# The delta-rule inverse and chunk loop of a two-block decoder, with TensorE's products, one low part and the gate products in another order

## The reference

```python
def step(state, inp):
    r_t, k_t, v_t, w_t, a_t, b_t = inp
    sa = jnp.einsum('bhvk,bhk->bhv', state, a_t)
    state = state * w_t[:, :, None, :] + sa[..., None] * b_t[:, :, None, :] + v_t[..., None] * k_t[:, :, None, :]
    return state, jnp.einsum('bhvk,bhk->bhv', state, r_t)
...
y = head_norm(y, gn_gain.reshape(H, N), RWKV_GN_EPS)
bonus = jnp.sum(rh * kh * r_k[None, None].astype(jnp.float32), axis=-1, keepdims=True) * vh
return (y + bonus).reshape(B, S, W) * g          # g = sigmoid(g_lo) @ g_up
```

## Time and profile before

| | us |
|---|---|
| median of three runs | 1006.78 |
| lowest, highest | 1005.49, 1008.01 |
| the profiled execution | 1008.22 |
| its span, first to last instruction | 1006.4 |
| TensorE busy in the span | 874.4 |
| VectorE busy | 451.5 |
| ScalarE busy | 331.8 |
| GpSimd busy | 17.4 |
| mean DMA rate over the span | 292 GB/s |

### The profile page before, as it was taken

The page is one execution under the profiler, slowest core; times in us unless marked ns, Lnnn a source line. Parts: engine busy times, 40 slices in busy tenths (PEclk is TensorE's granted clock), DMA queues, the critical chain, the costliest instruction groups (busy, mean ns, idle before and its releaser), DMA issues.

```text
span 1006.4 us, 16152 instructions
## 1 busy us (share of the span) xinstructions
PE 874.4 (87%) x6998; PEld 603.9 (60%) x6998; DVE 451.5 (45%) x579; ACT 331.8 (33%) x433; POOL 17.4 (2%) x34
## 2 busy tenths in 40 slices
PE   9999999999999999999899988666866776686785
PEld 7889988888888889989888633121312212131232
DVE  6776778678776448897766311000100000010002
ACT  6476664665555328645433300000000000000002
POOL 0420000000000000000000000000000000000000
PEclk9999999999999999999999999787979879789798
DMA  9894324576645455452369999999999999999995
GB/s 324 247 360 136 141 87 167 167 254 211 200 168 190 186 168 209 146 189 85 109 195 344 391 411 398 428 428 428 428 429 427 428 428 429 427 430 429 423 425 226
DMA packets 75968, 294.34 MB, mean 292 GB/s; under 512 B 5247, under 2 KB 32655, under 8 KB 62592
## 3 DMA queue, kind: packets, MB, share of 16 engines
q1 hardware_dynamic: 70352, 283.91, 72.5%
q10 hardware_dynamic: 4128, 6.34, 1.8%
q0 software_dynamic: 1424, 3.16, 1.1%
HBM read 290.25 MB, written 4.10 MB: 292 GB/s over the span
## 4 chain that ended last, share of the span: by engine, by line
PE 63%; DMA 28%; DVE 5%; issue 2%; SPq 1%; ACT 1%; DVEq 0%; ACTq 0%
DMA arena<-in_w_down 10%; DMA arena<-in_w_gate 9%; DMA arena<-in_w_up 8%; PE psum L1262 8%; PE psum L1950 8%; PE psum L1125 6%; PE psum L1126 6%; PE psum L1127 6%; PE psum L1289 4%; PE psum L1264 4%; PE psum L1978 3%; PE psum L1628 2%; PE psum L1162 1%; PE psum L1161 1%; PE psum L1159 1%
## 5 line engine op out<-in xcount | busy, mean ns | idle before, releaser
L1950 PE MATMUL psum<-arena,featL 128*32 128x512 f32 x1008 | 158.7, 697 | 58.4 <-DMA arena<-in_w_up 33.3
L2525 DVE TENSOR_TENSOR ring_rounded<-arena,hi_rounded 128x2048 fp32r<-128x2048 f32 x76 | 173.6, 2289 | 59.8 <-ACT hi_rounded L2077 58.6
L2077 ACT ACTIVATE hi_rounded<-arena 128x2048 fp32r<-128x2048 f32 x76 | 144.8, 1912 | 85.2 <-PE psum L1127 22.3
L1950 PEld LDWEIGHTS psum<-arena,featL 128*32 128x32 f32 x1008 | 37.7, 124 | 167.2 <-issue 86.6
L1262 PE MATMUL psum<-ffn_in_rounded,hi_rounded 128*128 128x512 f32 x352 | 122.4, 394 | 0.7 <-DVE ffn_in_rounded L2517 0.7
L1978 PE MATMUL psum<-arena,featT 128*32 128x512 f32 x424 | 79.1, 729 | 37.6 <-DMA arena<-in_w_down 33.2
L1125 PE MATMUL psum<-hi_rounded,featT_rounded 128*128 128x256 f32 (+1 forms) x336 | 104.1, 310 | 3.1 <-DVE featL_rounded L2567 2.2
L1127 PE MATMUL psum<-hi_rounded,featL_rounded 128*128 128x256 f32 (+1 forms) x336 | 101.8, 303 | 0.0
L1126 PE MATMUL psum<-ring_rounded,featT_rounded 128*128 128x256 f32 (+1 forms) x336 | 101.8, 303 | 0.0
L1264 PE MATMUL psum<-ffn_in_rounded,ring_rounded 128*128 128x256 f32 x352 | 97.5, 277 | 0.0
L1262 PEld LDWEIGHTS psum<-ffn_in_rounded,hi_rounded 128*128 128x128 f32 x352 | 66.0, 187 | 16.2 <-DVE ffn_in_rounded L2517 1.0
(11 more groups left out here) (367 smaller groups left out, 1278.7 us busy)
## 6 DMA issues: line engine op xcount, KB each, us to landing
arena<-in_w_down SPq DMA_DIRECT2D x32, 2048.0 KB, 17.1
arena<-in_w_gate SPq DMA_DIRECT2D x28, 2048.0 KB, 21.0
arena<-in_w_up SPq DMA_DIRECT2D x24, 2048.0 KB, 23.3
arena<-in_w_in SPq DMA_DIRECT2D x14, 2048.0 KB, 8.6
arena<-in_w_up SPq DMA_DIRECT2D x25, 1024.0 KB, 8.4
arena<-in_w_gate SPq DMA_DIRECT2D x14, 1024.0 KB, 5.5
arena<-in_w_down SPq DMA_DIRECT2D x7, 1024.0 KB, 10.8
arena<-in_w_out SPq DMA_DIRECT2D x3, 2048.0 KB, 8.2
```

Of the source, the lines that this page charges most:

```text
L1950: ins = mm(psum[32 * j:32 * j + 32, MB[4 + m], :], xg[:, 4 * half + k, 32 * j:32 * j + 32], weights(m, half, j, 512 * k), start=half == 0 ...
L2077: fn(high, view, ACT.Copy).then_inc(hi_ready, 1)
L2525: tt(low, view, high.bitcast(F32), ALU.subtract).then_inc(lo_ready, 1)
```

## The change

It computes the same values. TensorE's order and the fill list are written anew between 467 and 530 us, and what ACT, DVE and SP do about those fills follows.

- `natl A` (eight transposes) moves from the start of mixing to between Re and Ro; `gn` moves from behind Q to behind Aak; Q moves from before TT to behind it. AakT gets another place in SBUF (`AakT = P2`, in featT).
- `u_inner(1)` and `u_inner(2)`, and `y_rows(0)` and `y_rows(1)`, are merged so that products of the two chunks alternate. `mT 0 0` moves from before `u_inner(0)` to behind `u_state(1)`, `mT 1 0` from before `u_state(3)` to behind the last `y_rows`.
- The low part of the second `wo2` chunk is made by GpSimd.
- `gated_bonus` for both t and `gated_gain(0)` stand before the loop, `gated_gain(1)` in its first turn. `low_moved` of `mT 0 0` stands in turn 1, that of `mT 1 0` behind `rw_square(1)`, and ACT's `y_moved(1)` and `high_moved` of `mT 1 0` stand before its first `root`.
- The pieces that SP loads wait for other fills.

```diff
 (fill list)
+BETWEEN = {"H3": (("mat", "Aak"), ("gn",)), "N": (("mat", "Re"), ("natl", "A"), ("mat", "Ro")), "TT": (("Q",),)}
 (SP)
-                    first_load(NQ, 0, ("inv", "N", 1), ("mat", "Ro", 1), *inv(("HT", 0), ("HT", 1)))
+                    first_load(NQ, 0, ("gn", 1), ("inv", "N", 1), ("mat", "Ro", 1), ("inv", "HT", 1))
...
-                    first_load(3, 2, ("St", 0), ("U", 1, 1), ("St", 1), ("U", 2, 1))
+                    first_load(3, 2, ("U", 1, 1), ("St", 1), ("U", 2, 1), ("St", 2))
 (GpSimd)
+            g = chunk_of[("wo2", 0), 1]
+            pool.wait_ge(hi_ready, g + 1)
+            pool.wait_ge(lo_ready, g)
+            high, view, low = hi_view(g)
+            ptt(low, view, high.bitcast(F32), ALU.subtract).then_inc(lo_ready, 1)
 (TensorE)
+                if name == "H3":
+                    mat("Aak")
+                    for t in range(NT):
+                        b = begin("gn", t)
+                        pe.wait_ge(lora_act, 2)
+                        end(mm(b, sig_g[:, t * P:(t + 1) * P], gup[:], start=True, stop=True))
+                if name == "N":
+                    mat_both("Re", 0)
+                    for t in range(NT):
+                        transposes(("natl", "A", t), [At[:, k, t * P:(t + 1) * P] for k in range(4)],
+                                   lambda: pe.wait_ge(rw_ready, 1))
+                    mat_both("Ro", 1)
...
+                for i in range(4):
+                    for par in range(2):
+                        for c in chunks:
+                            t, r, to, h = c // 2, head_rows(c % 2), head_rows(1 - c % 2), 2 * i + par
+                            ins = mm(banks[c][par][to, 64 * i:64 * i + 64], TT[r, t, 4 * par + i, :], Qn[r, t, 64 * h:64 * h + 64],
...
             state(0)
-            u1 = u_inner(1)
-            u2 = u_inner(2)
+            u1, u2 = u_inner(1, 2)
             u_state(u1, 1)
+            transposes(("mT", 0, 0), mixed_rows(0, 0), lambda: pe.wait_ge(mixed_ready, 1))
+            state(1)
             y0 = [begin("Y", 0, par) for par in range(2)]
-            y_rows(y0, 0)
-            state(1)
             y_state(y0, 1, True)
             u_state(u2, 2)
-            y_rows(y0, 1)
+            u3, = u_inner(3)
             state(2)
-            u3 = u_inner(3)
-            transposes(("mT", 1, 0), mixed_rows(1, 0), lambda: pe.wait_ge(mixed_ready, NT))
+            y_rows(y0, 0, 1)
             u_state(u3, 3)
...
             y_rows(y1, 3)
+            transposes(("mT", 1, 0), mixed_rows(1, 0), lambda: pe.wait_ge(mixed_ready, NT))
 (ScalarE)
                 if c == 2:
                     y_moved(0)
-                    high_moved("mT", 1, 0)
+            y_moved(1)
+            high_moved("mT", 1, 0)
             root(48, RW_H, 64, 2)
-            y_moved(1)
             high_part(first["wo2", 0] + 2, ("Y", 1, 1))
 (VectorE)
-                    low_part(chunk_of[("wo2", 0), 1])
...
+            gated_bonus(0)
+            gated_bonus(1)
+            gated_gain(0)
             for c in range(NCH):
...
                 if c < NCH - 1:
+                    if c == 1:
+                        low_moved("mT", 0, 0)
                     if c:
                         link(tt(S[c + 1], S[c], bc(PC[:, :, c], 64), ALU.mult))
                     wait_filled(dve, "St", c)
...
                     if c == 0:
                         empty(nc.vector.tensor_copy(S[1], b), "St", 0)
-                        gated_bonus(0)
+                        gated_gain(1)
...
-            gated_bonus(1)
             rw_square(0)
-            gated_gain(1)
             rw_scale(0)
             rw_square(1)
+            low_moved("mT", 1, 0)
             rw_scale(1)
```

More of the change, by code:

```diff
@@ L266, in plan_fills @@
     add("act", "p2", 3, 1)
-    for t in range(NT):
-        add("act", "natl", "A", t)
     for j in range(3):
@@ L1521, in _ @@
             tokens_late(("p2", 3, 1), ("p2", 3), 1)
-            for t in range(NT):
-                transposes(("natl", "A", t), [At[:, k, t * P:(t + 1) * P] for k in range(4)], lambda: pe.wait_ge(rw_ready, 1))
             for j in range(3):
@@ L1708, in y_state, with y_rows @@
                             ins.then_inc(y_first, 1)
[L1710 to L1712 removed]
+            def y_rows(banks, *chunks):
                 for name in ("Re", "Ro"):
                     wait_emptied(pe, "mat", name, 1)
[L1715 to L1717 removed]
+                for c in chunks:
+                    u_known(c)
+                    if c:
+                        pe.wait_ge(y_first, 2 * c)
                 for i in range(4):
                     for par in range(2):
[L1720 to L1724 removed]
+                        for c in chunks:
+                            t, both, h = c // 2, (Re, Ro)[c % 2], 2 * i + par
+                            ins = mm(banks[par][head_rows(c % 2), 64 * i:64 * i + 64], both[:, t, 4 * par + i, :],
+                                     VU[c][:, 64 * h:64 * h + 64], start=c == 0 and i == 0, stop=True, skip_group_check=True)
+                            if c % 2 and i == 3:
+                                end(ins)
             u_inner(0)
@@ L2327, in _ @@
             ret_move(3, 1)
-            for t in range(NT):
-                wait_filled(act, "natl", "A", t)
-                empty(fn(natl["A"][:, t, :], bank("natl", "A", t), ACT.Copy), "natl", "A", t)
             high_part(first["wo2", 0], ("p2", 3, 1))
@@ L2363, in _ @@
                     high_part(first["wo2", 0] + 1, ("p2", 3, 1))
+                if name == "H3":
+                    for t in range(NT):
+                        wait_filled(act, "gn", t)
+                        empty(fn(gnat[:, t, :], bank("gn", t), ACT.Copy), "gn", t)
                 if name == "N":
                     root(48 + RET_H, RET_H, RET_D, 1)
+                    for t in range(NT):
+                        wait_filled(act, "natl", "A", t)
+                        empty(fn(natl["A"][:, t, :], bank("natl", "A", t), ACT.Copy), "natl", "A", t)
                 if name == "TT":
-                    high_moved("mT", 0, 0)
-                if name == "G2":
                     for t in range(NT):
@@ L2371, in _ @@
                         empty(fn(Qn[:, t, :], bank("Q", t), ACT.Copy), "Q", t)
-                    for t in range(NT):
-                        wait_filled(act, "gn", t)
-                        empty(fn(gnat[:, t, :], bank("gn", t), ACT.Copy), "gn", t)
             def y_moved(t):
@@ L2927, in _ @@
                     merge()
-                for e in INV_EXTRA.get(name, ()):
-                    for par in range(2):
-                        masked(extra[e][0], e, extra[e][1], par)
+                for key in BETWEEN.get(name, ()):
+                    if key[0] == "mat":
+                        dst, m = extra[key[1]]
+                        for par in range(2):
+                            masked(dst, key[1], m, par)
+                        if key[1] == "Re":
+                            ret_scale(0)
                 if name == "H3":
```

89 lines of the change are left out of this document (29 added, 60 removed).

## The result

The changed kernel takes **1009.24 us** (median of 14 runs, 1007.75 to 1011.27), the kernel before 1007.12 (14 runs beside them, 1005.49 to 1008.84). The ratio is 1.002, with a 95% interval of 1.0011 to 1.0028: some 2 us slower. The forecast was 1006.0 with a range up to 1008.6. So the two traces end at the same time, and the difference has to be read from where each stage starts.

The account below looks back on a forecast made before the run. The prediction took the experts' weight transfers as the bound, released by mixed_ready = 4 and the wo2 fills. Terms -1.1 (issue), -0.6 (mT 0 0), +0.25 (loop), +0.7 (end of mixing) gave -0.75, or -0.8 us: 1006.0, range 1003.4 to 1008.6.

Parts of the forecast that it names:

- What bounds the kernel: Experts' weight transfers bound the end; it moves only with mixed_ready = 4 and the end of the wo2 fills.
- The issue waits: -1.1: In the inverse: light work moved among the products saves 1.1 us of TensorE's 3.52 us of instruction waits; bounds 0 and 3.5.
- The count by blocks of 4.15 us: In the inverse: instructions arrive in blocks of some 127 products with weight loads, one per 4.15 us at best.
- rival 2: In the inverse: the issue waits only move, saving 0, sum +0.3, 1007.1 us; chance 0.10.
- the 0.55 near Re: In the inverse: third of five issue waits, to vanish since gn, N and Re take 5.0 us, above 4.15.
- the 0.32 and the 0.46: In the inverse: first and last of five issue waits; 0.32 was to stay, 0.46 to stay as 0.3 to 0.5.
- mT 0 0 leaves: -0.6: Before the loop: removing mT 0 0's transposes saves 0.6 us; with the issue waits the loop starts at 513.35 us.
- The loop: +0.25: Chunk loop: alternating saves 0.6 and 0.6, a new 1.2 us wait before u_state(2) takes it; 0.25 us longer.
- The end of mixing: +0.7: From u_state(3): VectorE waits 2.4 us for ACT's root; 0.7 given back, mixed_ready = 4 comes 0.75 earlier.
- The wo2 products see the same: In the wo2 stage: despite waiting for mT 1 0's low part, the first fill ends 0.7 to 0.8 us earlier.
- rival 3: In the wo2 stage: TensorE's clock falls to half behind a 2.6 us wait, 3.0 us lost, 1009.0; chance 0.05.
- Rival 4: Beside H2 and H3: GpSimd's low part holds VectorE up, at most 3.5 us lost, 1009.5; chance 0.05.

Follow-up runs that it names:

- before_mt: Kernel before with only mT 1 0's transposes, high part and low part moved to the end of mixing as in the change; ratio 1.0007.
- tail_loop: Changed kernel with t = 0's root first, mT 1 0's low part right behind t = 0's scaling, mT 0 0 behind state(1), its low part behind the state sum; ratio 1.0001.
- late_pieces: Changed kernel with SP's 1-MB pieces of experts' weights held back until U of the last chunk is full; 1017.12 us.
- gate_alt: Kernel before with the gate products moved from behind U3, and u_inner(1, 2) and y_rows(0, 1) alternating, u_inner(3) ahead of state(2); ratio 0.9991.
- changed_again: The changed kernel itself run once more, unaltered, against the kernel before; ratio 1.0019.
- filler9: Changed kernel with 9 products of no use put into TensorE's stop of 2.53 us in the wo2 stage; ratio 1.0004.
- low_first: Changed kernel with VectorE's low part of mT 1 0 moved ahead of the scaling of t = 0; ratio 1.0010.
- gate_tail: gate_alt with mT 1 0's transposes behind the last y_rows, t = 0's root first on ACT, mT 1 0's low part right behind t = 0's scaling; ratio 0.9970.
- gate_tail_shift: gate_tail with one of SP's 1-MB loads, (2, 2), moved from beside TT and Q to behind load (3, 1); ratio 0.9964, 1004.05 us.

## Why the prediction was wrong, step by step

**What bounds the kernel: right, and not followed to its end.** I named two events, mixed_ready = 4 and the end of the fills. The runs speak for the second as the mark: the change and before_mt are early at the first (0.23, 1.16 us) and late at the second (1.58, 0.66), and neither is faster. It is no perfect mark: tail_loop is early at both and its median is not, and from the second issue to the end of the span the 17 traces of the table take 458.8 to 462.5 us.

**"The issue waits: -1.1": wrong.** The count by blocks of 4.15 us gave each stretch the same supply. It forecast 0.1 each for TT and Q; Q had 1.48 and state(0) 0.79 and 0.23. That is rival 2 (the waits only move), which had 0.10. Two things were missing: that fetches are slower beside weight transfers (late_pieces), and that gn and mT 0 0 stood in just that stretch, where they hid the fetch. The count was good in the first half: the 0.55 near Re is gone and 0.35 of the 1.24 is left, as forecast (0.35 to 0.65); the 0.32 and the 0.46, which were to stay, have left the chain too. But there VectorE's work leads the chain, and G1 waits 0.30 for it, a term that I did not have.

**"mT 0 0 leaves: -0.6": right for the removal**, but with the waits the loop starts 1.04 us earlier and not 1.7.

**"The loop: +0.25": nearly right in size.** The loop from u_inner(0) to u_state(3) is 0.44 longer (11.59 against 11.15). The wait before u_state(2) is 1.02 (1.2 forecast), ended by VectorE's state sum, the pair 1.17 (1.05), y_rows 0.93 (1.4). The 1.02 us of issue waits in state(0) and behind it were not in the walk. gate_alt shows the alternation by itself: nothing gained.

**"The end of mixing: +0.7": right in kind, too large.** VectorE's gap ended by ACT's root is 2.26 (2.4). u_state(3) to first issue takes 11.57 against 11.20, so 0.37 is given back. mixed_ready = 4 comes 0.23 earlier instead of 0.75.

**"The wo2 products see the same": the step that failed.** I passed the shift of mixed_ready on to the fills, 0.7 to 0.8 us earlier. Instead the stage took 9.24 us between the two issues, where the kernel before takes 7.43, so 1.81 were lost. Two things make them up. The order costs 0.52: TensorE has a turn and two groups of products more behind its stop, and is nearly full from 534.78 on, so what sets the second issue is when mT 1 0's low part comes, and no longer mixed_ready. Even without a fall it would have come at 545.12, 0.3 later than before. The clock costs 1.29, by the two traces of the change. This is rival 3, in its place and from the wait that it named. Its price was 3.0, since I let the low clock last until 557 us and it lasted until 538.6; its chance was 0.05. That its 1009.0 lies beside the 1009.24 measured is luck: the clock gave 1.3 of it, and the rest is in the terms above. Against it stood one stop of 2 us at 1.00, and I took it for a rule. In ten traces the clock fell behind one of four stops of 2.2 us and five of six of 2.5 or 2.6.

**Rival 4: no**, and the rule of the Trainium skill that was set beside it (SBUF — State Buffer, who interferes with whom) agrees in the half that this kernel shows: sums with one input in PSUM keep their 0.69 us beside GpSimd's 4.53. No VectorE op with two SBUF inputs ran in that time. GpSimd's price was 3.5; it is 4.53, inside the bounds.

**Instruction fetch.** The profile's section on queues lists the fetches as transfers of their own, in every run:

```profile
q8 instruction: 50, 0.82, 0.3%
```

That is 16 KB each. The Trainium skill (Runtime: NRT & Kernel Launch, instruction fetch mechanics) calls the cost mostly hidden; 2.2 to 4.7 us in the chains of all runs at full loads say otherwise here, and 1.07 in the change with the loads held back say when it comes nearer to the truth (2.34 in the kernel before).

**The sum.** By the second issue: start of the loop -1.04, loop +0.44, end of mixing +0.37, which is -0.23 at the first issue; then +1.81 in the wo2 stage, 0.52 of it the order and 1.29 the clock. That makes +1.58; measured +2.1 (1.1 to 2.8). The scatter of the loop's own clock, seen in changed_again, may be the rest; it was not measured apart.

Why do the two profiled executions end together, then? The kernel before has 349 GB/s from 610 to 620 us, the change 400:

```profile
610.00:620.00 10.00, 6.47 (x56) 2.80 (x48) 0.69 (x1) 0.60 (x1) 0.00 (x0) 1.00 0.90 349
```

There SP waits for TensorE to free places of the ring (issue at 617.27, in the change at 617.35), and TensorE had the low clock from 602 to 608 in that execution. By the rates of windows of 5 us, summed, the change is 1.4 us of transfers behind at 600 us and 0.1 at 620: the kernel before lost its lead there. What this stretch does varies too: from 602 to 608 us the two traces of the change have 0.72 and 0.56. A single trace of each would have said "no difference"; the repeated runs do not.

**Open.** What decides whether a stop of 2.2 us drops the clock. Whether the 1.29 us of the clock reach the end in full: they are read at the second issue, and in the time filler9's 1.6 us are no larger than the noise. How often the clock falls here in runs without a trace. How much of tail_loop's scatter comes from the loop.

## What to carry to other kernels

Before an engine is given a longer wait, look at what the clock does behind waits of that length in several executions, and price the slower products behind it: here a stop of 2.5 us in place of 2.2, for one low part of 0.7 us that now came behind the loop, was followed by a fall that cost TensorE 1.3 us. Count also how much of its work an engine has in front of a wait and how much behind it; that cost 0.5 here without any fall. Light work moved to cover one wait for instructions can uncover another: the change closed 2.67 us of them and opened 2.30. Mark several events on the way to the end, not one: the first was early and the second late.

## What the runs showed of the hardware that I had not expected

- Issue waits went with the DMA engines' other traffic: from Q to u_inner(1), in the change's order, 2.23 to 3.84 us with all loads (seven runs), 1.67 and 1.38 with one 1-MB load less beside them, 0.30 with none (single traces). With the inverse of the kernel before, 3.72, 2.90 and 2.69 in all with the loads, 2.34 without.
- TensorE's clock fell to 0.50 behind six of ten stops of 2.2 to 2.6 us and behind none of nine of up to 1.3 us, after the same dense work; in the loop it fell behind issue waits of 1.34, 2.22 and 2.71 us, but stayed at 1.00 behind waits of 1.48 in Q (the change, low_first) and 1.51 in HT (gate_tail, gate_tail_shift).
- A stretch at 0.50 was some 3 us long, and over 6 in filler9, with TensorE busy nearly throughout. One of them in the wo2 stage put the second issue 1.29 us later.
- GpSimd subtracts 128x2048 in float32 in 4.53 us, VectorE in 2.28.
